# Third output tile inside the entries, squares summed by column groups, score products in pairs of key blocks

## What is computed

```
x = x + 0.5 * rmsnorm(swiglu(rmsnorm(x)))      feed-forward, 1024 -> 2816 -> 1024
x = x + rmsnorm(hybrid_mixer(rmsnorm(x)))      1024 -> 1440 inputs, attention, -> 1024
x = x + 0.5 * rmsnorm(swiglu(rmsnorm(x)))      feed-forward
x = x + rmsnorm(emb * sigmoid(rmsnorm(x) @ w)) gate on a per-layer embedding ("Ple")
rmsnorm(v) = v * rsqrt(mean(v*v) + 1e-6) * gain
```

## Time and profile before

| | us |
|---|---|
| median of 3 runs | 3004.22 (3003.27 to 3006.89) |
| the profiled execution | 3005.28 |
| its span | 3003.5 |
| PE busy | 2862.1 (95%) |
| DVE busy | 1558.5 (52%) |
| ACT busy | 1145.5 (38%) |
| POOL busy | 243.3 (8%) |

### The profile page before, as it was taken

How to read it: one execution, slowest core, us unless ns; L and a number is a source line. 1 busy time by engine, 2 the same in 40 slices (tenths; PEclk the granted TensorE clock), 3 DMA queues, 4 the chain that set the end, 5 groups by cost and what they waited for, 6 DMA issues and landing times.

```text
span 3003.5 us, 42576 instructions
## 1 busy us (share of the span) xinstructions
PE 2862.1 (95%) x17236; PEld 2384.8 (79%) x17236; DVE 1558.5 (52%) x2618; ACT 1145.5 (38%) x1861; POOL 243.3 (8%) x272
## 2 busy tenths in 40 slices
PE   6999889899999999999999999899999999999997
PEld 3866888778788888777888888788888778888886
DVE  5744465544354434855644436644436755644346
ACT  3333444243333323455433224532324564333234
POOL 0000065400000000200000000000000201000000
PEclk7999999999999999999999999999999999999998
DMA  6222000022232332301222332233332301332321
GB/s 237 64 67 73 3 8 3 15 91 92 77 106 98 98 106 92 117 32 50 72 97 98 99 106 78 77 98 99 98 105 96 95 29 43 98 98 93 104 91 57
DMA packets 69778, 244.92 MB, mean 82 GB/s; under 512 B 8464, under 2 KB 10640, under 8 KB 68944
## 3 DMA queue, kind: packets, MB, share of 16 engines
q1 hardware_dynamic: 69584, 242.21, 24.5%
HBM read 234.70 MB, written 3.15 MB: 79 GB/s over the span
## 4 chain that ended last, share of the span: by engine, by line
PE 67%; DVE 3%; ACT 2%; issue 1%; DVEq 0%; ACTq 0%
PE pair L228 20%; PE pair L230 20%; PE pair L229 20%; PE pair L2568 2%; PE pair L2597 2%; PE pair L357 2%; PE pair L2607 1%; ACT w_hi_at L182 1%; DVE rstd_at L473 1%; DVE work_at L308 0%; DVE w_lo_at L190 0%; PE pair L491 0%; DVE residual L314 0%; DVE h_lo_at L319 0%; PE pair L488 0%
## 5 line engine op out<-in xcount | busy, mean ns | idle before, releaser
L228 PE MATMUL pair<-h_hi_at,w_hi_at 128*128 128x512 f32 (+1 forms) x2048 | 781.3, 381 | 35.9 <-DVE h_lo_at L319 31.4
L229 PE MATMUL pair<-h_lo_at,w_hi_at 128*128 128x512 f32 (+1 forms) x2048 | 759.1, 371 | 0.0
L230 PE MATMUL pair<-h_hi_at,w_lo_at 128*128 128x512 f32 (+1 forms) x2048 | 759.0, 371 | 0.0
L190 DVE TENSOR_TENSOR w_lo_at<-w_raw,w_hi_at 128x1024 fp32r<-128x1024 f32 x348 | 439.4, 1263 | 430.6 <-ACT w_hi_at L182 430.4
L182 ACT ACTIVATE w_hi_at<-w_raw 128x1024 fp32r<-128x1024 f32 x348 | 364.8, 1052 | 523.5 <-PE pair L230 512.1
L228 PEld LDWEIGHTS pair<-h_hi_at,w_hi_at 128*128 128x128 f32 x2048 | 389.0, 190 | 112.2 <-DVE h_lo_at L319 37.4
L229 PEld LDWEIGHTS pair<-h_lo_at,w_hi_at 128*128 128x128 f32 x2048 | 389.1, 190 | 67.1 <-issue 0.5
L230 PEld LDWEIGHTS pair<-h_hi_at,w_lo_at 128*128 128x128 f32 x2048 | 388.9, 190 | 65.3
L2330 DVE TENSOR_TENSOR work_at<-pair,rstd_at 128x512 f32<-128x512 f32 (+1 forms) x184 | 122.1, 667 | 363.2 <-PE pair L230 363.1
L228 PE MATMUL pair<-a_hi_at,w_hi_at 128*128 128x512 f32 (+1 forms) x792 | 290.1, 366 | 0.0
L229 PE MATMUL pair<-a_lo_at,w_hi_at 128*128 128x512 f32 (+1 forms) x792 | 289.4, 365 | 0.0
(11 more groups left out here) (423 smaller groups left out, 3975.8 us busy)
## 6 DMA issues: line engine op xcount, KB each, us to landing
w_raw<-in_weights SPq DMA_DIRECT2D x431, 512.0 KB, 3.4
residual<-in_x SPq DMA_DIRECT2D x1, 2048.0 KB, 12.0
cos_sin_at<-rope_table SPq DMA_DIRECT2D x2, 1024.0 KB, 4.8
by_sin_at<-delta_at SPq DMA_DIRECT2D x32, 64.0 KB, 2.0
by_sin_at<-kd_at SPq DMA_DIRECT2D x32, 64.0 KB, 2.0
out<-residual SPq DMA_DIRECT2D x16, 128.0 KB, 1.7
q_wide<-in_ctx SPq DMA_DIRECT2D x1, 1024.0 KB, 12.9
rope_table<-zb SPq DMA_DIRECT2D x1, 1024.0 KB, 4.2
```

The source lines that it names most:

```text
L190: eng.tensor_tensor(self.w_lo[:, g % self.split].rearrange("p k n -> p (k n)"), self.w_raw[:, g % RAW], self.w_hi[:, g % self.split].rearr ...
L228: pe.matmul(out, sh, mh, start=start, stop=False)
L229: pe.matmul(out, sh, ml, start=False, stop=False)
L230: return pe.matmul(out, sl, mh, start=False, stop=stop)
```

## The change

- `Entry` has a third output tile. `pe_product(n, m)` multiplies block n into tile m; tile 2 runs three blocks behind (`BEHIND`). Both halves of a tile now share one bank, and DVE drains a tile in one instruction. The gate's entry keeps two tiles.
- Squares are summed four blocks at a time (`pe_sums`): four matmuls with 32 columns of ones, each into 32 partitions of its own of the sum bank. ACT copies the partial sums (`act_partial`), and PE folds them with the 128x128 matrix of ones (`pe_fold`). The root's scale has a factor of 32 more.
- ACT squares one block behind its rounding. `w_make_hi` and `w_make_lo` of the third tile's granule move to the third block and to DVE's step 3; the fourth tile's take their old place. In the stages behind, each is made one granule further ahead. DVE makes the first half's reciprocal ahead of a granule's low part.
- The PSUM banks of tiles are dealt out anew, some waits for drains go with that, and the mixer's exit sums its first half in the last tile but one.
- The window attention's score products take two key blocks at once where two follow in a pair.

```diff
-    FIRST_BANKS = ((0, 1), (6, 7))
+    FIRST_BANKS = (0, 1, 7)
+    BEHIND = 3
 ...
-    def act_tile(self, act, half, t):
+    def act_round(self, act, half, t):
 ...
+    def act_square(self, act, half, t):
+        n = half * KD + t
         if n >= 4:
-            act.wait_ge(*self.summed(n - 3))
-        act.activation(self.sq[:, n % 4], x[:, t, c], ACT.Square).then_inc(self.squared.sem, 1)
+            act.wait_ge(*self.summed(n // 4))
+        act.activation(self.sq[:, n % 4], self.kit.residual[:, t, cols(half)], ACT.Square).then_inc(self.squared.sem, 1)
+    def act_partial(self, act, half):
+        act.wait_ge(*self.summed(2 * half + 2))
+        act.activation(self.partial[:, cols(half)], self.kit.banks[self.SUM_BANK[half]][:, 0:HALF],
+                       ACT.Copy).then_inc(self.part_copied.sem, 1)
     def act_root(self, act, half):
-        act.wait_ge(*self.summed(KD * (half + 1)))
+        act.wait_ge(*self.folded(half + 1))
 ...
+    def pe_sums(self, pe, batch):
+        half, second = divmod(batch, 2)
+        pe.wait_ge(*self.squared(4 * batch + 4))
+        for q in range(4):
+            last = pe.matmul(self.kit.banks[self.SUM_BANK[half]][32 * q:32 * q + 32, 0:HALF], self.kit.square("ones")[:, 0:32],
+                             self.sq[:, q], start=not second, stop=bool(second), skip_group_check=True)
+        last.then_inc(self.summed.sem, 1)
+    def pe_fold(self, pe, half):
+        pe.wait_ge(*self.part_copied(half + 1))
+        pe.matmul(self.kit.banks[self.SUM_BANK[half]][:, HALF:], self.kit.square("ones"), self.partial[:, cols(half)],
+                  start=True, stop=True).then_inc(self.folded.sem, 1)
 ...
     def pe(self, pe):
-        for half in range(2):
-            for t in range(KD):
-                self.pe_products(pe, half, t)
-                if self.leave and half == 0 and t == 1:
-                    self.leave.pe_sum(pe, 1)
-                if t >= 1:
-                    self.pe_sum(pe, half, t - 1)
-            self.pe_sum(pe, half, KD - 1)
+        for n in range(2 * KD):
+            if n in (4, 8, 12):
+                self.pe_sums(pe, n // 4 - 1)
+            for m in range(2):
+                self.pe_product(pe, n, m)
+            if self.leave and n == 1:
+                self.leave.pe_sum(pe, 1)
+            if n >= self.BEHIND:
+                self.pe_product(pe, n - self.BEHIND, 2)
+            if n == 10:
+                self.pe_fold(pe, 0)
+        self.pe_sums(pe, 3)
+        for n in range(2 * KD - self.BEHIND, 2 * KD):
+            self.pe_product(pe, n, 2)
 ...
     def act(self, act, made):
 ...
-                self.act_tile(act, half, t)
+                self.act_round(act, half, t)
                 if half == 0 and t == 1 and leave:
                     leave.act_late(act)
+                if half == 0 and t == 2:
+                    kit.w_make_hi(act, self.g0 + 2)
                 if half == 0 and t == 3 and leave:
                     leave.act_squares(act, 1)
                 if half == 0 and t == 4:
                     if leave:
                         leave.act_root(act, 1)
-                    kit.w_make_hi(act, self.g0 + 2)
+                    kit.w_make_hi(act, self.g0 + 3)
                 if half == 1 and t == 1:
+                    self.act_partial(act, 0)
+                if half == 1 and t == 3:
                     self.act_root(act, 0)
+                if t >= 1:
+                    self.act_square(act, half, t - 1)
+            self.act_square(act, half, KD - 1)
+        self.act_partial(act, 1)
         self.act_root(act, 1)
 ...
-        makes = {KD: lambda: kit.w_make_lo(dve, self.g0 + 2)}
+        makes = {3: lambda: kit.w_make_lo(dve, self.g0 + 2), KD: lambda: kit.w_make_lo(dve, self.g0 + 3)}
 ... window attention
-                                pieces=[(kb, j * P) for j, (kb, _) in enumerate(blocks)], values=[vb for _, vb in blocks],
+                            pieces = [(ka[:, b * P:(b + len(blocks[j:j + 2])) * P], j * P)
+                                      for j, b in enumerate(blocks) if j % 2 == 0]
 ... Ffn
-    BANKS = ((0, 1), (3, 2))
+    BANKS = ((0, 1), (7, 4), (3, 6))
+    DOWN_BANKS = (5, 7, 4, 2)
+            for which in range(f == 1, 2):
+                    if f == 1 and k == 1:
+                        self.entry.pe_fold(pe, 1)
-                if half == 0 and k == 0:
-                    pe.wait_ge(*self.out_stored(4))
-                if half == 1 and k == 0:
-                    pe.wait_ge(*self.out_stored(5))
 ... Mixer
-    RING = (3, 2, 0, 1, 6, 7)
+    RING = (0, 1, 7, 3, 2, 0, 1, 6, 7, 3, 2, 0)
-            kit.w_used, self.o0 + t + 1) if half else self.half_done(t - self.full + 1)) for t in (KD - 2, KD - 1)])
+            kit.w_used, self.o0 + t + 1) if half else self.half_done(2)) for t in (KD - 2, KD - 1)])
+                if t == 3 and k == 1:
+                    self.entry.pe_fold(pe, 1)
-                    if half == 1 and t == KD - 1 and k == 1:
+                    if half == 1 and t == KD - 2 and k == 2:
                         self.exit.pe_sum(pe, 0)
-            kit.w_make_hi(act, g0 + t + 3)
+            if t < self.TILES - 1:
+                kit.w_make_hi(act, g0 + t + 4)
+                self.entry.dve_rstd(dve, 0)
+                kit.w_make_lo(dve, g0 + 4)
+                self.entry.dve_rstd(dve, 1)
+                dve.wait_ge(*self.entry.rstd_ready(2))
 ... Ple
-    EMB_BANKS = (0, 1, 3, 6)
+    EMB_BANKS = (0, 1, 4, 7)
+        for n in range(2 * KD):
+            for m in range(2):
+                self.entry.pe_product(pe, n, m)
+            if n == 0:
+                self.entry.pe_sums(pe, 1)
+            if n == KD + 2:
+                self.entry.pe_fold(pe, 0)
+            if n == KD + 4:
+                self.entry.pe_sums(pe, 2)
+        self.entry.pe_sums(pe, 3)
+                if t == 2 and k == 2:
+                    self.entry.pe_fold(pe, 1)
```

More of the change, by code:

```diff
@@ L360, in pe_products @@
-    def pe_products(self, pe, half, t):
-        kit, c = self.kit, cols(half)
-        pe.wait_ge(*self.h_ready(half * KD + t + 1))
-        for m in range(2):
-            if half == 0 and t == 0:
-                pe.wait_ge(kit.w_split, self.g0 + m + 1)
-            last = matmul3(pe, kit.banks[self.FIRST_BANKS[half][m]][:, 0:HALF], kit.w_tile(self.g0 + m, t),
-                           (self.hi[:, t, c], self.lo[:, t, c]), t == 0, t == KD - 1)
-            if half == 1 and t == KD - 1:
-                last.then_inc(kit.w_used, 1)
@@ new lines, in dve_rstd @@
+    def dve_rstd(self, dve, half):
+        dve.wait_ge(*self.rooted(half + 1))
+        dve.reciprocal(self.kit.rstd[:, cols(half)], self.kit.rstd[:, cols(half)]).then_inc(self.rstd_ready.sem, 1)
+    def pe_sums(self, pe, batch):
[5 more added lines that the diff above has]
+        last.then_inc(self.summed.sem, 1)
@@ L2502, in pe @@
         self.entry.pe(pe)
-        for t in range(2, self.TILES):
-            if t == 3:
+        for t in range(3, self.TILES):
+            if t == 4:
                 pe.wait_ge(*self.entry.rooted(2))
-            if t >= 4:
-                pe.wait_ge(*self.drained(t - 3 if t < 6 else max(t - 5, 2)))
+            if t >= 5 and t != 7:
+                pe.wait_ge(*self.drained(max(i for i in range(t) if self.RING[i] == self.RING[t]) + 1))
             if t == 4:
@@ L2840, in dve @@
                    b["kd"][:, t - 8])
-            for bank, c in self.entry.first_parts(t) if t < 2 else [(self.bank(t), slice(0, SEQ))]:
-                last = dve.tensor_tensor(dst[:, c], bank, kit.rstd[:, c], ALU.mult)
-            last.then_inc(self.drained.sem, 1)
+            dve.tensor_tensor(dst, self.bank(t), kit.rstd[:, :], ALU.mult).then_inc(self.drained.sem, 1)
+            if 0 < t < self.TILES - 1:
+                kit.w_make_lo(dve, g0 + t + 4)
         for r in (6, 7):
@@ L2990, in pe @@
                 self.before.exit.pe_sum(pe, 1)
-            if t == 1:
-                pe.wait_ge(*self.before.out_stored(KD - 2))
-            if t >= 1:
-                self.entry.pe_sum(pe, 0, t - 1)
+            if t == 5:
+                self.entry.pe_sums(pe, 0)
         pe.wait_ge(*self.emb_drained(KD))
-        for half in range(2):
-            for t in range(KD):
-                self.entry.pe_products(pe, half, t)
-                if half == 0 and t == 0:
-                    self.entry.pe_sum(pe, 0, KD - 1)
-                if half == 1 and t >= 1:
-                    self.entry.pe_sum(pe, 1, t - 1)
-        self.entry.pe_sum(pe, 1, KD - 1)
+        for n in range(2 * KD):
+            for m in range(2):
+                self.entry.pe_product(pe, n, m)
+            if n == 0:
+                self.entry.pe_sums(pe, 1)
[4 more added lines that the diff above has]
+        self.entry.pe_sums(pe, 3)
         for t in range(2, self.full):
@@ L3112, in dve @@
                 dve.wait_ge(*self.gated(t - 1))
```

(5 more changed lines are left out.)

106 lines of the change are left out of this document (59 added, 47 removed).

## The result

The changed kernel took 3020.18 us (median of 4 runs, 3019.18 to 3025.59), the kernel before, run beside it, 3003.74 (4 runs). The ratio is 1.0052, 95% interval 1.004 to 1.0063: slower, by 16.4 us. The forecast was 3002.1. Further down, one of the six runs of the kernel called repaired took 3956.7 us at a mean granted clock of 0.673: its ratio leaves that run out, and its median is 2993.42 without it, 2993.90 with it.

A forecast was written before the change was run, and what follows sets the result against it. TensorE was taken as the bound, busy 2862.1 of 3003.5 us, with DVE level in the entries. Gains 0.9 - 6.1 + 6.8 - 1.0 + 0.0 + 1.5 = 2.1; 3005.28 - 1.06 - 2.1 = 3002.1 us, range 2982 to 3010.

The forecast's parts named there:

- The gate's entries: Gate's two entries: sums save 2.8, later weights and rounds leave 1.0, the fifth tile's low part 1.0 late: 0.0.
- The clock behind the new gaps: Entries after a feed-forward or mixer: the forecast priced no clock fall behind the new PE gaps of about 2.6 us.
- The second rival: Clock falls to 1.2 GHz behind the first block's 2.6 us gap in four entries: 5.9 us more, 3008.0; chance 0.24.
- tile 6's gap: Behind the mixer's entry: PE waits 2.35 us before tile 6 for the latents' roots, behind granule 9's high part.
- The mixers' -3.05 each: Mixer entry and tiles: 0.2 lost in the entry plus new waits ahead of tiles 4 and 6; -6.1 for both.
- The mixer exit's +3.4: Mixer's exit, twice: first-half sum 2.5 us earlier, clock gives back 1.3, less 0.2 and 0.2; +6.8 for both.
- The 1.3 us that the clock was to give back: Behind the mixer's exit: PE's gap shrinks from 3.5 to 1.1, so the clock stays up, less slow products and sum.
- Layer 1's first feed-forward, -1.0: Entry after the gate: a gap of 3.05 before block 3 becomes one of 4 before block 1, 1.0 us lost.
- First block and entry, +2.4: Start to first feed-forward's down products: window scores gain 1.5, layer 0's first feed-forward entry about 0.9.
- The batch, 0.8: Entries: four column-group sums cost PE 0.57 to the next matmul plus 0.2 in it, both changes of width included.
- The bound of 1.72: Entries: upper bound in us for a batch if its four sums run one after another.
- The first rival: Third tile hides the added waits and PE's work decides: 25 us gained with the latents' wait kept, 2979; chance 0.22.

The follow-up runs named there:

- repaired: Changed kernel with gate_batch, roots_first, root_late and lo3_late joined, both reciprocals ahead of the fifth granule's low part, gate batches and squares moved: 2993.90 us, 0.9954 of before.
- gate_batch: Changed kernel with the gate's first batch of sums issued behind the fifth embedding tile instead of the sixth: 3013.82 us, 1.0035 of the kernel before.
- root_late: Changed kernel with ACT's root of the first half two rounds later in every entry: 3013.29 us, 1.0019 of the kernel before.
- repaired_2: repaired plus lo2_next and, in the gate, the fourth and fifth granules' high parts ahead of the second half's root and first sigmoid: 2976.20 us, 0.9905 of before.
- roots_first: Changed kernel with ACT taking the latents' two roots ahead of tile 9's high part in the mixer: 3013.30 us, 1.0022 of the kernel before.
- before_parts: Kernel before with only the mixer exit's first sum one tile earlier and window scores two key blocks to a matmul: 2998.27 us, 0.9972 of before.
- lo2_next: Changed kernel with DVE making the third tile's granule's low part one step later in feed-forward and mixer entries: 3007.11 us, 1.0006 of the kernel before.
- whole_sums: Changed kernel with each batch's four sums through the whole array, accumulated, without partial copy and fold: 3026.72 us, 1.0072 of the kernel before.
- two_tiles: Changed kernel with the third output tile taken out of feed-forward and mixer entries and multiplied whole behind them: 3027.70 us, 1.0076 of the kernel before.
- lo3_late: Changed kernel with DVE making the fourth granule's low part behind the activations' last low part in feed-forward and mixer entries: 3013.68 us, 1.0018 of before.

## Why the prediction was wrong, step by step

The profiled spans missed the forecast by 16.5 us (14.4 measured, -2.1 forecast), the medians by 18. Two steps carry it: the gates with 8.8 and the clock behind the new gaps with 6.0; the rest is 1.7 of an attention without an edit.

- **The gate's entries, forecast at 0.0 each, cost 3.7 and 5.1 us: this step failed.** It said that the weights would come 1 us earlier than before. The first product came 15.22 us behind the first embedding product, for 15.17 before: not earlier at all. The wait ahead of it grew by 2.42 us (0.25 to 2.67) and took up all that PE's shorter sums had saved, as the square that waits for the first batch stands ahead of the embedding copies on ACT. The step had the rounds "behind fold, root and batch", but priced the fifth block's delay and the fold's stand of 5.91 us on ACT at less than what the sums save. The savings were real; they were overtaken. gate_batch and root_late moved one of the two holes each and got 0.4 and 1.6 us back (both with layer 1's first feed-forward); it took both with the squares moved (repaired) to bring the two gates back to 150.3 us for the 150.1 of before (gate 1: 74.97 us from the first embedding product to the last sum, for 73.78; 72.33 in repaired_2). Which of repaired's edits in the gate did how much is open. I had not walked ACT's queue through the gate instruction by instruction as I had in the mixer.
- **The clock behind the new gaps, put at nothing in the forecast, cost 6.0 us: this step failed too.** The second rival had it: "The clock falls in the gap after the first block". It fell to 0.50 in all four places that the rival names, in both mixers' entries and in both entries behind the mixers, and behind tile 6's gap in layer 0, which the rival did not have. The forecast for the two mixers and the stretches behind them is -0.7 in sum, the measurement +5.3. The rival's price was 5.9; that it meets the 6.0 so closely is in part luck, since some 1.6 of these lie behind tile 6's gap. The rival read from the earlier trace rows that gaps up to 1.62 leave the clock up; the trace of before had a counter-example, the gate's 1.58 in layer 0. No run holds the clock up by design: its price is read where the same code kept it.
- **The mixers' -3.05 each was -5.6 and -4.5.** The longer waits were right within 0.1 us (2.51, 0.43, 2.41); the one on the fold was 0.50 for 0.7, and those for `h_lo` ahead of blocks 4 and 6 were 0.41 and 0.93 for 1.0 and 1.1. Where the clock stayed up (gate_batch's second mixer) the whole is 3.27, so the sum was right and the clock is what it lacked. roots_first shows the price of tile 6's wait with its consequences: 4.7 and 2.4.
- **The mixer exit's +3.4 was +2.0 and +2.9.** The move itself did what was forecast (the gap 0.79, clock up), and where the clock also survived the next gap (roots_first, layer 0) the stretch gave 3.5. before_parts shows the move worth 3.5 and 4.8 alone. The 1.3 us that the clock was to give back was lost a block later, in the entry's own gap of 2.50. lo2_next, which removes the gap, gives back 3.4 and 3.8 us there.
- **Layer 1's first feed-forward, -1.0**: 254.50 to 255.50 us, right.
- **First block and entry, +2.4**: 2.36 in sum, but not by its own terms. 0.8 of it was there before the first entry began, 0.7 of that in the window's scores for 1.5 forecast, in a stretch that moves by several us from one profile to the next. The feed-forward's entry and tiles gave 1.5 for 0.9, but in before_parts, with the code of before, they gave 1.1. This sum is not shown to be right.
- **The batch, 0.8**: 0.74 (0.57 to the next product, 0.17 in those behind), right. The rule of the Trainium skill, "TensorEngine Tiling (Array Packing)", Key Properties, that changing the tiling mode drains the array agrees with that pair, where the bare batch was put at 0.43. The bound of 1.72 for four sums one after another is near whole_sums' 1.54 to the next product.
- **Mixer 0's attention, +1.66, not forecast**: no edit lies in it. Its mean granted clock was 0.96 after and 0.99 before. In seven of the twelve experiments' profiles attention of one layer (in roots_first of both) took 1.5 to 3.5 us more than its usual 136.2, in either layer; in the two kernels with the old entries (before, before_parts) it did in neither. Whether that is chance stays open.

The first rival, that the third tile hides the new waits and PE's work decides, was wrong for this kernel. Its price, 2979 us, is near the 2976.2 of repaired_2, but that is no test of it: repaired_2 keeps some waits and removes others that the kernel before had. What I had against that rival was that each order is fixed in the code; so it was, and a few of these orders, none of which touches what is computed, were the whole difference between a loss of 16 us and a gain of 28.

## What to carry to other kernels

Where work is moved forward on one engine, walk the queue of every other engine instruction by instruction in each stage that shares the code, and ask of each instruction that waits what stands behind it that the critical engine needs first; a root, a square or a weight's part that can wait goes behind what can't. Measure the parts alone, in the kernel before as well: here the smallest edit (one sum in an earlier tile) paid at once, and the two large ones, each worth some 7 us in the changed kernel and 13 and 14 in the repaired ones, were hidden by the orders around them. A PE gap of some 2.5 us costs its own length and mostly another 1.5 us or so in clock, so shorten the longest gap first, and put a chance on the clock when you price one.

## What the runs showed of the hardware

- Four fp32 sums through the whole array, one behind another, take 1.54 us to the next product, and by four column groups 0.57. A single one among products moves the next by 0.25, but makes its block 0.43 longer.
- A gap of the same length, in the same code, did not always bring the clock down. Seven profiles keep the wait of 2.41 us ahead of tile 6 in both mixers (after, gate_batch, two_tiles, whole_sums, root_late, lo3_late, lo2_next). Behind 8 of these 14 gaps the clock fell to 0.50, and the stretch from tile 4 to the first latent product took 51.2 to 51.4 us; behind 6 it stayed at 1.00 and the stretch took 49.8 to 49.9. Two windows of lo2_next show both, layer 0 first:

```profile
1221.00:1224.00 3.00, 2.30 (x10) 1.97 (x11) 3.00 (x2) 2.09 (x4) 0.00 (x0) 1.00 0.00 0
...
2319.00:2323.00 4.00, 3.07 (x8) 2.48 (x9) 4.00 (x2) 2.32 (x4) 0.00 (x0) 0.57 0.00 0
```

  What tells them apart the runs don't show. In or behind the gap of 2.50 us in the entries it fell in 25 of 28 (the first six of these kernels and roots_first), and the gate's 1.58 us before did it in one layer and not in the other.
- The start of the program, up to the first feed-forward's down products, varied between 1047 and 1057 us over the profiles. Differences of a few us between two kernels are read stretch by stretch or not at all.
